# Three of eight row pairs with seven block products instead of two, and two sums in one operation, in a two-block transformer kernel

## The reference

```python
for l in range(2):
    h = _rms_norm(x, norm_g[l])
    proj = jnp.einsum('bsd,de->bse', h, w_in[l])      # 2048 -> 6208 columns
    q_a, k_a, v_a, z_a, c_q, c_kv, k_r, z_b = jnp.split(proj, split_points, axis=-1)
    # differential attention on q_a, k_a, v_a; latent attention on c_q, c_kv, k_r; gates z_a, z_b
    x = x + jnp.einsum('bse,ed->bsd', mixed, w_out[l])
```

## Time and profile before

| | |
|---|---|
| median of 3 runs | 1917.46 us (1917.41 to 1917.61) |
| profiled execution | 1917.76 us |
| its span, first to last instruction | 1915.6 us |
| PE busy | 1906.9 us, 100% |
| DVE busy | 1429.9 us, 75% |
| ACT busy | 1071.7 us, 56% |
| PE clock granted | 0.999 of 2.4 GHz |
| moved by DMA | 361.38 MB |

### The profile page before, as it was taken

One profiled execution on the slowest core, in us unless ns is written; L12 is line 12 of the kernel. 1 busy time (PEld: TensorE's weight loads), 2 busy tenths in 40 slices (PEclk: granted clock), 3 DMA queues, 4 the chain that ended last, 5 costly groups with the idle time before them and its releaser, 6 DMA issues.

```text
span 1915.6 us, 26983 instructions
## 1 busy us (share of the span) xinstructions
PE 1906.9 (100%) x9951; PEld 1627.5 (85%) x9951; DVE 1429.9 (75%) x1996; ACT 1071.7 (56%) x1586; POOL 48.7 (3%) x72
## 2 busy tenths in 40 slices
PE   9999999999999999999999999999999999999998
PEld 8888898888888898888888888888888888888886
DVE  6777675656777675655768766888878887889898
ACT  6655675655545676654644444555555555555554
POOL 1000030000000030000100000000000000000000
PEclk9999999999999999999999999999999999999999
DMA  9864545565665456545666455666666666665654
GB/s 342 303 217 133 148 151 161 166 207 178 216 205 164 145 156 192 152 159 185 211 191 186 152 176 177 189 183 187 196 188 190 191 186 187 190 223 192 204 194 172
DMA packets 260363, 361.38 MB, mean 189 GB/s; under 512 B 15504, under 2 KB 159072, under 8 KB 259760
## 3 DMA queue, kind: packets, MB, share of 16 engines
q1 hardware_dynamic: 258400, 353.15, 58.6%
q0 software_dynamic: 1584, 6.67, 1.0%
q10 hardware_dynamic: 288, 0.33, 0.1%
HBM read 356.95 MB, written 3.16 MB: 188 GB/s over the span
## 4 chain that ended last, share of the span: by engine, by line
PE 99%; DMA 0%; ACT 0%; DVE 0%; SPq 0%; issue 0%; DVEq 0%; ACTq 0%
PE acc L471 22%; PE acc L464 12%; PE acc L448 10%; PE acc L449 10%; PE acc L450 10%; PE acc L1281 3%; PE acc L1552 3%; PE acc L1554 3%; PE acc L1553 3%; PE acc L1261 3%; PE acc L1260 3%; PE acc L1259 3%; PE acc L1284 2%; PE aux L541 1%; PE acc L491 1%; PE aux L1552 1%
## 5 line engine op out<-in xcount | busy, mean ns | idle before, releaser
L411 DVE TENSOR_TENSOR sb_w_lo<-sb_stage,sb_w_hi 128x1024 fp32r<-128x1024 f32 x476 | 582.2, 1226 | 267.2 <-ACT sb_w_hi L406 260.3
L406 ACT ACTIVATE sb_w_hi<-sb_stage 128x1024 fp32r<-128x1024 f32 x476 | 503.2, 1058 | 380.4 <-PE acc L464 122.7
L471 PE MATMUL acc<-sb_xT,sb_w_hi 128*128 128x512 f32 x1856 | 445.8, 392 | 0.0
L471 PEld LDWEIGHTS acc<-sb_xT,sb_w_hi 128*128 128x128 f32 x1856 | 341.1, 188 | 65.5
L464 PEld LDWEIGHTS acc<-sb_xT,sb_w_lo 128*128 128x128 f32 x1856 | 238.7, 191 | 9.3
L464 PE MATMUL acc<-sb_xT,sb_w_lo 128*128 128x256 f32 x1856 | 243.1, 284 | 0.0
L448 PE MATMUL acc<-sb_w_hi,sb_mT 128*128 128x512 f32 x480 | 191.1, 398 | 0.0
L449 PE MATMUL acc<-sb_w_lo,sb_mT 128*128 128x512 f32 x480 | 187.3, 390 | 0.0
L450 PE MATMUL acc<-sb_w_hi,sb_mT 128*128 128x512 f32 x480 | 187.2, 390 | 0.0
L448 PE MATMUL acc<-sb_w_hi,sb_xT 128*128 128x512 f32 x384 | 154.7, 403 | 0.0
L449 PE MATMUL acc<-sb_w_lo,sb_xT 128*128 128x512 f32 x384 | 150.1, 391 | 0.0
(11 more groups left out here) (493 smaller groups left out, 3026.0 us busy)
## 6 DMA issues: line engine op xcount, KB each, us to landing
sb_stage<-w_in SPq DMA_DIRECT2D x232, 512.0 KB, 4.4
sb_stage<-w_up SPq DMA_DIRECT2D x176, 512.0 KB, 3.7
sb_stage<-w_out SPq DMA_DIRECT2D x96, 512.0 KB, 4.2
sb_stage<-w_down SPq DMA_DIRECT2D x54, 512.0 KB, 6.6
sb_pair_stage<-w_down SPq DMA_DIRECT2D x34, 512.0 KB, 5.4
sb_kvb<-w_in SPq DMA_DIRECT2D x16, 512.0 KB, 6.3
sb_stage<-w_ukv SPq DMA_DIRECT2D x16, 512.0 KB, 4.1
sb_stage<-w_kv SPq DMA_DIRECT2D x15, 512.0 KB, 6.7
```

Source lines behind the costliest of these rows:

```text
L406: act.activation(w_hi[:, j % RING, 0:size], stage[:, j % RING, 0:size], ACT.Copy).then_inc(hi_ready, 1)
L411: dve.tensor_tensor(w_lo[:, j % RING, 0:size], stage[:, j % RING, 0:size], w_hi[:, j % RING, 0:size].bitcast(F32), ALU.subtract).then_inc( ...
L471: mm = pe.matmul(acc[:, 2 * pair + c, :], hi[:, k, c * P:(c + 1) * P], both, start=first and k == 0, stop=last and k == 3)
```

## The change

`QKV_ITEMS` now takes pair 2 as a seven too: rows of pairs 3 and 4, seven 0, rows of 5, seven 1, seven 2, rows of 6 and 7: 22 units a third, 60 in the stage instead of 56. `mix_x(2)` is added in DVE's iteration 13 of each layer, and `seven_x` is one pair longer. The lead of three units lasts to unit 11 and grows to five at units 12 and 13 (before: at 8 and 9); the turning of the slots follows. The load of a pair whose seven directly follows another is issued one row load earlier. The sums b11 + b12 and b12 + b22, which share b12, are one operation of 2 x 512 elements, here and in the stage of w_down.

```diff
-U_QKV = 56
+U_QKV = 60
...
-QKV_ITEMS = 2 * [[[2, 3, 4], 0, [5], 1, [6, 7]]]
-QKV_MIXED = 2
+QKV_ITEMS = 2 * [[[3, 4], 0, [5], 1, 2, [6, 7]]]
+QKV_MIXED = 3
...
-QKV_TURNED = 8
-QKV_SLOT = [(j + (2 if j >= QKV_TURNED else 0)) % QKV_RING for j in range(U_QKV)]
+QKV_TURNED = (8, 12)
+QKV_SLOT = [(j + 2 * sum(j >= turned for turned in QKV_TURNED)) % QKV_RING for j in range(U_QKV)]
...
-    first = {0: [3], 1: [4], 2: [5], 3: [6], 4: [7], 5: [8], 6: [9], 7: [10], 8: [11, 12], 9: [13, 14]}
+    first = {**{j: [j + 3] for j in range(12)}, 12: [15, 16], 13: [17, 18]}
...
# rest_down and rest_qkv, the same in both:
-                step(dve.tensor_tensor(b11, b11, b12, ALU.add))
-                dve.tensor_tensor(b12, b12, b22, ALU.add).then_inc(qkv_sums_ready, 1)
+                dve.tensor_tensor(pair[:, :, 0:512], pair[:, 0, :].rearrange("p (a n) -> p a n", a=2), again(b12, 2),
+                                  ALU.add).then_inc(qkv_sums_ready, 1)
...
                         for n, first in enumerate(QKV_SEVENS[:-1]):
-                            if first + 4 == j:
+                            follows_pair = QKV_SEVENS[n + 1] == first + 4
+                            if j == (first - 1 if follows_pair else first + 4):
                                 load_qkv_pair(n + 1)
...
-                        if j in (5, 9):
-                            mix_x(j // 8)
+                        if j in (5, 9, 13):
+                            mix_x(j // 4 - 1)
```

More of the change, by code:

```diff
@@ L789, in rest_down @@
                 dve.wait_ge(lo_ready, U4 + (j + 1))
-                step(dve.tensor_tensor(b11, b11, b12, ALU.add))
-                dve.tensor_tensor(b12, b12, b22, ALU.add).then_inc(sums_ready, 1)
+                dve.tensor_tensor(pair[:, :, 0:512], pair[:, 0, :].rearrange("p (a n) -> p a n", a=2), again(b12, 2),
+                                  ALU.add).then_inc(sums_ready, 1)
                 dve.wait_ge(sums_ready, 2 * sevens_until(j) - 1)
```

## The result

The changed kernel takes 1923.1 us (median of 9 runs, 1921.76 to 1924.69) where the kernel before, run beside it, takes 1917.45 (9 runs, 1916.88 to 1918.31): 1.0030 times, 95% interval 1.0020 to 1.0041. The forecast was 1914.8, range 1914.2 to 1917.2. The profiled execution has a span of 1921.3 us, 5.7 more than before.

What follows compares the result with a forecast made beforehand. PE's matmul count was taken to bound the kernel: 12 fewer give -2.72 us, all else +0.0, so 1917.46 becomes 1914.7, or 1914.8 with a tenth or so at unit 38; range 1914.2 to 1917.2.

Steps and rivals of the forecast that it cites:

- What bounds the kernel, and what 12 matmuls are worth: Whole kernel: PE's count of matmuls sets the time; 12 fewer at 0.2267 us save 2.72 us.
- DVE's work per seven, the merged sum, two sevens in a row: Keys stage: 6.99 us of DVE per seven, merged sum 1.23 us; PE doesn't wait, 1.3 us spare at unit 32.
- The start of the stage ... Cost nothing: Layer 0, units 12 and 13: iteration 13's extra DVE work, including the third mix (3.05 us), is hidden; cost nothing.
- that string: DVE from PE's start of unit 13: rest of 18 done at 2.5 us, extra work 8.3, rest of 19 9.6.
- Even a load that lands 5 us late is hidden: Start of the stage: rest of 19 done at 9.6 us after unit 13's start, PE wants it at 16.5.
- Unit 38: Start of the next third: PE may wait for banks 0 and 1; landing of 5.6 us means 1.5 us per layer.
- 0.37 us is left: Unit 38, each layer: banks 0 and 1 free at 41.11 us after unit 16's start, PE needs them at 41.48.
- nearly empty: Unit 38's load: five loads issued some 8 us earlier leave the engines nearly empty, so it lands in 3.7 to 3.9 us.
- This rival: PE waits for banks at unit 38 if the landing exceeds 4.1 us; total 1916.0 to 1917.7; chance 0.21.
- The rival of the other sign: Merged sum at half rate, 2.45 us, in keys and w_down stages: +4.5 us, 1922; chance 0.05 shared with another wait.
- 0.05 for "slower": Whole kernel: chance of half rate or another wait making it slower; over 0.2% slower needs 6.5 us of new waits.
- One sign: A break in PE's pitch at the first seven of layer 0 would mean the third mix comes too late.

Runs made afterwards that it cites:

- the runs without it: Pair 3 issued behind the row load of 37, on the kernel with the addition before the rest of 21: 1915.69 us; also pairs 4, 3 swapped: 1915.37; or additions in iteration 35: 1914.61.
- the base of the last runs: The changed kernel with the last query pair's addition in DVE's iteration 16, before the rest of unit 21 and the sums: 1915.94 us, ratio 0.9991.
- the version without waits in the stage: Base with addition before the rest of 21, plus pair 3 issued behind row load of 37 and additions for banks 0 and 1 in iteration 35: 1914.61 us.
- the kernel with the gap of 2.41 us: The changed kernel with the last query pair's addition before the rest of unit 22 instead of behind it: 1919.09 us, ratio 1.0009.

## Why the prediction was wrong, point by point

- **What bounds the kernel, and what 12 matmuls are worth: right.** Forecast 2.72 us; once PE waits nowhere in the stage, measured 2.8 and 2.9 by medians and 2.6 and 2.8 by spans. By the 131 ns for a matmul that the Trainium skill gives ("TensorE: Matmul & The Clock Gate", section Back-to-back issue gap) it would have been an estimated 1.6 us; these runs don't bear that out.
- **DVE's work per seven, the merged sum, two sevens in a row: right.** The merged sum took 1.225 us for the 1.23 taken, and no run shows a wait at units 20 to 34. The rest of unit 34 came when forecast: with the addition before the rest of 21, SyncE issued the load of unit 38 at 124.31, 28.9 us after PE's start of unit 16 (95.45).
- **"The start of the stage ... Cost nothing": this step failed.** It followed the rests from iteration 13 on and compared them with PE's use of the same units. At this place it never asked about the other thing that DVE hands to PE, the banks, though it did at unit 38. I counted "the addition of a query pair (0.61)" as work and did not follow what it releases. The addition of iteration 17, which frees banks 2 and 3, was not looked at, nor that the list now wants them at unit 18. The rows at hand would have given the first part of it: 22's rest cannot be done earlier than 2.5 us after PE starts 17, the banks are wanted after 2.72, and the addition of 0.69 has to fit between, so PE waits some 0.5 us in each layer (0.62 measured with the mix moved away). The larger part came from DVE's own lateness behind the mix. It cost 3.67 + 0.11 us in layer 0 and 1.65 in layer 1, and moving the addition gave it all back.
- **The times of that string were too short as well.** Forecast was the rest of unit 19 ready 9.6 us after PE's start of unit 13. In the changed kernel that start is 87.27 (95.64 less 3 x 2.79) and the rest ends at 97.30 + 1.22 = 98.52, 11.2 us behind it. The forecast let ACT round unit 18 after 0.26 us; ACT went with it at 89.31, 2.0 us behind, because it rounded 17 first, from 87.93 on, and then waited 0.3 us for the load. "Even a load that lands 5 us late is hidden" held for the rest of 19 itself (PE wanted it at 103.8), but not for the addition behind it. In layer 1 DVE stood idle for 0.99 us before the rest of 18, which waited for a load of 4.75 us; no run took that load's lateness away by itself.
- **The clock was no term of the sum.** A gap of 3.67 us cost 1.67 more in pitch. With the waits left out, so was this.
- **Unit 38: the mechanism was right, the size near.** "0.37 us is left" at a landing of 3.7 us; the landings were 4.2 us in layer 0 and 5.1 in layer 1 (issues at 129.96 and 568.19, ACT at 134.17 and 573.29), the waits 0.2 and 1.07 with the first matmul. I had 1.5 for a landing of 5.6. That 38 would find the engines "nearly empty" was wrong in layer 0: the batch behind pair 3 was still landing, and in the runs without it the load took 3.6 to 3.8 us. This rival alone would have ended at about 1915.9, the base of the last runs.
- **The rival of the other sign** had a price near the result (1922) but a mechanism that does not exist here. That its price was near is luck, and counts for nothing.
- **Chances.** 0.05 for "slower" rested on one mechanism and "another wait". With a list reordered in every layer, and three kinds of thing that PE waits for (rests, mixes, banks), two of them followed only in part, that was too little. One sign came near: a break at the first seven of layer 0 was to mean that the third mix comes too late; it came two units ahead of the seven, and the mix made most of it.

## What to carry to other kernels

When a list of work is reordered, write down for each engine not only the data that it hands over but everything that it releases (banks, slots, buffers), with who wants it first in the new order; an operation of 0.7 us whose result nobody waits for may be the one that frees the accumulator. A release that stands behind other work in an engine's list inherits all of that work's waits, so a release that another engine wants soon goes ahead of work that can wait. And where PE is the bound, price a gap by the gap and, if it is long (3.67 us here), by what the clock may take after it.

## What the runs showed of the hardware

After a gap of 3.67 us PE ran at a granted clock of 0.50 for 3.4 us and lost 1.67 us more; after one of 3.70 us, in the run with two sums, the clock was at 0.50 from about the first matmul on, also for 3.4 us. After a gap of 2.41 us and after those of 1.54 us and less it did not fall in the profiled executions. Where the gap was long the runs also scattered more: 2.9 us between the lowest and highest of the changed kernel and 3.7 with the addition before 22, against 0.9 for the version without waits in the stage. Whether the clock fell in the slower runs of the kernel with the gap of 2.41 us isn't shown: there is one trace of it. The first matmul after a wait for banks has 0.33 or 0.34 us to the next instead of 0.23, and 0.60 where the clock was low already.
